# Two of four weight-splitting subtractions at the end of a decoder step move from VectorE to GpSimd

## The chip, the core and the metric

The kernel runs on one core of a Trainium2 chip. The core has TensorE (matmuls), VectorE, ScalarE and GpSimd (elementwise work), and SyncE, which issues most of the transfers; each works through a queue of its own, and they meet at semaphores. The metric is the device time of one execution in microseconds; the median of several is compared.

## What is computed

One layer of a hybrid decoder for 544 tokens (512 of a prompt and 32 of running sequences), model width 1024, all in float32. It ends with a mixture of experts and a gated embedding:

```python
x = x + mix
x = x + moe(rmsnorm(x, norm_ffn), w_router, b_router, w_up, b_up, w_down, b_down)
x = x + jax.nn.sigmoid(x @ w_ple_gate) * (p.astype(x.dtype) @ w_ple_proj)
...
y_prompt = rmsnorm(xp, norm_final)
```

The change lies around the line with `w_ple_gate`, a matrix of 1024x1024. In `moe` every token is sent to 4 of 32 experts, and the four results are weighted and added.

## The kernel before

**Split products.** A float32 product is made of faster fp32r products. A weight chunk `raw` is split: ScalarE copies it into a high part of type fp32r (`w_hi`, `gate_hi`), and VectorE subtracts that from `raw` for the low part (`w_lo`, `gate_lo`). TensorE then multiplies high by high, high by low and low by high, into the same PSUM banks.

**The experts.** The tokens (five tiles: four of 128 rows, one of 32) are gathered in blocks of 128 rows by expert. For each block 12 chunks of weights (1 MB each, 128 partitions x 2048) stream from HBM into a ring of six slots `raw`, eight for the first matrix and four for the second. A block's result goes through ScalarE into `y_rows` (line 887), and GpSimd scatters it into the table `expert_rows` in HBM by an indirect transfer (line 714). The index column `scatter_col` for it is written by VectorE (line 1635), once the scatter before has landed.

**The tail.** After the last block's steps the order is written out by hand in each engine's program:
- SyncE loads the four chunks of the gate matrix into ring slots 0 to 3 (line 579). When the last scatter has landed, it loads four rows of results per token from the table, in two halves for each tile (line 586): `yk0`, which lies in the ring slots 4 and 5 and is named `raw` in the profile, and `yk1`.
- ScalarE makes the last `w_hi` (line 849), then `gate_hi0` to `gate_hi3` (line 919) with `y_rows` and the copies `ple` between them.
- VectorE makes the last four `w_lo` (line 1541), waits for TensorE's last expert matmul, and makes the four `gate_lo` (line 1744). Between them stand `b_down_add(1)` and `b_down_add(2)` (line 1728), which add a bias sum that TensorE made in PSUM (line 1306) to `resid`. Then comes `combine(0)` (line 1763): four operations that add the weighted results of one token tile to `resid`. `gate_lo` lies in the memory of the ring slots 0 to 3, so each part overwrites its chunk.
- TensorE makes the last expert matmuls (lines 1207 and 1216), embedding products (line 1157) and bias sums (line 1306), and then, for each token tile, transposes of `resid` (line 1341, waiting for `combine`) and the gate products (lines 456, 458 and 465). Before the first of them it waits for all of `gate_hi` (semaphore `s_ghi`) and `gate_lo` (`s_glo`).
- GpSimd issues the last two scatters and then makes five tiny `rstd` operations (line 739), one for each tile, for the last norm.

Of the kernel before, what the change touches and what calls it, by code (L numbers as in the profile page):

```python
# [22 lines left out]
F32 = mybir.dt.float32  # L23
# [3 lines left out]
ALU = mybir.AluOpType  # L27
# [7 lines left out]
DN_CHUNKS = 4  # L35
# [5 lines left out]
def build(nc, x_prompt, x_sample, state_pool, p_prompt, p_sample, norm_mix, w_in, w_pool, pool_scale,  # L41
# [36 lines left out]
    with ctx:  # L78
        def sb(name, shape, dt=F32, scope=ctx):
            return scope.enter_context(nc.sbuf_tensor(name, shape, dt))  # L80

        def sem(name):
            return ctx.enter_context(nc.semaphore(name))
# [60 lines left out]
        with ExitStack() as s:  # L144
            raw = sb("raw", [P, RING, 2 * FF], scope=s)
        with ExitStack() as s:
            gate_lo = sb("gate_lo", [P, KD, D], F32R, scope=s)
# [100 lines left out]
        with ExitStack() as s:  # L248
# [7 lines left out]
            gate_hi = [sb(f"gate_hi{i}", [P, 2, D], F32R, scope=s) for i in range(2)]  # L256
# [33 lines left out]
        JOBS += [(("rank", 0), "V"), (("count", 0), "V"), (("slots", 0), "V"), (("ple", 0), "A"), (("gatesT", 0), "V")]  # L290
        assert TT == 5 and all(n % 4 != 3 for n in range(len(JOBS) - 2, len(JOBS)))
        JOB = {name: n for n, (name, _) in enumerate(JOBS)}
        EMPTIED = {}
        for n, (name, who) in enumerate(JOBS):
            EMPTIED[name] = sum(w == who for _, w in JOBS[:n + 1])
        TOTAL = {who: sum(w == who for _, w in JOBS) for who in "AV"}

        s_job = sem("job_filled")
# [92 lines left out]
        s_ghi = sem("gate_weights_hi")  # L391
        s_glo = sem("gate_weights_lo")
# [23 lines left out]
        def tail_banks(what, t):  # L416
            n = TAIL_BANK[what, t]
            return ps[:, n:n + 2, :]
# [180 lines left out]
        def _(pool):  # L599
# [109 lines left out]
            def scatter(u):  # L709
                ready = u + 1 if isinstance(u, int) else pool.to_reg(u + 1)  # L710
                pool.wait_ge(s_route, 1)
                pool.wait_ge(s_stage, ready)
                pool.wait_ge(s_y, ready)
                pool.indirect_dma_start(y4_dram[:, :], bass.IndirectOffsetOnAxis(ap=scatter_col[:, 0:1], axis=0),  # L714
                                        y_rows[:], None,
                                        bounds_check=last_row, oob_is_err=False).then_inc(s_scat, 16)

            def step(J):
                pool.wait_ge(s_stage, J if isinstance(J, int) else pool.to_reg(J))
                gather(J + 2, gather_col[:, 0:1])  # L720
                scatter(J - 1)
# [9 lines left out]
            with pool.If(n_over > 0):  # L731
                with pool.Fori(0, OVER) as b:
                    with pool.If(b < n_over):
                        step(b + (E - 1))
            scatter(n_over + (E - 2))
            scatter(n_over + (E - 1))
            for t in range(TT):
                pool.wait_ge(s_var3, t + 1)
                pool.tensor_tensor(rstd3[:, t:t + 1], var3[:, t:t + 1], half_neg[:, 0:1], ALU.pow).then_inc(s_rstd3, 1)
# [614 lines left out]
        def _(dve):  # L1354
# [93 lines left out]
            n = DB * PB  # L1448
# [276 lines left out]
            def b_down_add(t):  # L1725
                dve.wait_ge(s_bdp, t + 1)
                n = NT[t]
                dve.tensor_tensor(resid[0:n, t, :], resid[0:n, t, :], tail_banks("bd", t)[0:n].rearrange("p a n -> p (a n)"),
                                  ALU.add).then_inc(s_bd, 1)
# [9 lines left out]


            dve.wait_ge(s_lused, n_over * STEP_CHUNKS + E * STEP_CHUNKS)
            for c in range(DN_CHUNKS):
                dve.wait_ge(s_ghi, c + 1)
                dve.tensor_tensor(gate_lo[:, 2 * c:2 * c + 2, :].rearrange("p j n -> p (j n)"), raw[:, c, :],
                                  gate_hi[c][:].rearrange("p j n -> p (j n)").bitcast(F32), ALU.subtract).then_inc(s_glo, 1)
                if c % 2 == 1:
                    b_down_add((c + 1) // 2)
            tail = [0]

            def tlink(ins):  # L1750
# [78 lines left out]
```

## Time and profile before

| | us |
|---|---|
| median of three timed runs | 1469.86 (1469.83 to 1472.62) |
| the profiled execution | 1467.52 |
| its span, first to last instruction | 1465.7 |
| TensorE busy | 1419.8 |
| VectorE busy | 1225.4 |
| ScalarE busy | 927.9 |
| GpSimd busy | 210.2 |

The busy times come from one profiled execution; times inside it are counted from the start of its span. They are averages over unlike stages. The change touches only the last 100 us, so the timelines of the engines there are what has to be read. A timeline row gives start, duration, engine, line, operation, and in brackets how long the engine had stood still before and what released it. Rows of several like instructions are merged, with their count behind the x.

### The profile page before, as it was taken

The numbers are of one execution on the slowest core, as the hardware profiler recorded it, in microseconds if no ns is written. First come the engines' busy times: TensorE is split into PE (matmuls) and PEld (weight loads), VectorE is DVE, ScalarE is ACT, GpSimd is POOL, SyncE is SP. The second block draws the span as 40 slices with busy tenths as digits, with TensorE's granted clock in tenths as the row PEclk, the third lists the DMA queues.
The fourth block names the chain that finished last, engine by engine and source line by source line (L and its number), as shares of the span: only waits on it lengthen the run. The fifth ranks groups of instructions, "written<-read, shape, count | busy, mean of one in ns | idle before, by whom it ended". The sixth has DMA issues, their size and how long they took to land.

```text
span 1465.7 us, 19344 instructions
## 1 busy us (share of the span) xinstructions
PE 1419.8 (97%) x6527; PEld 1137.0 (78%) x6527; DVE 1225.4 (84%) x981; ACT 927.9 (63%) x630; POOL 210.2 (14%) x131
## 2 busy tenths in 40 slices
PE   6999978999999999999999999999999999999896
PEld 3795546888888888888888888888888888888485
DVE  2741448999999999999999999999999999999784
ACT  4310234777777777777777777777777777777422
POOL 3041000011111111111111111111111111111100
PEclk9999979999999999999999999999999999999999
DMA  9014245899999999999999999999999999999540
GB/s 313 1 61 156 73 161 222 326 362 365 383 367 374 373 371 366 369 372 369 369 369 369 370 369 371 372 376 377 373 372 376 375 374 366 367 367 362 211 173 36
DMA packets 94024, 457.31 MB, mean 312 GB/s; under 512 B 13298, under 2 KB 14878, under 8 KB 60069
## 3 DMA queue, kind: packets, MB, share of 16 engines
q1 hardware_dynamic: 84111, 437.50, 78.4%
q0 software_dynamic: 9360, 17.85, 3.2%
q10 hardware_dynamic: 526, 1.60, 0.4%
q8 instruction: 17, 0.28, 0.1%
q14 instruction: 10, 0.08, 0.0%
HBM read 451.76 MB, written 21.58 MB: 323 GB/s over the span
## 4 chain that ended last, share of the span: by engine, by line
PE 93%; DVE 2%; DMA 2%; issue 1%; ACT 1%; SPq 0%; DVEq 0%; POOLq 0%; POOL 0%; ACTq 0%
PE ps L1207 47%; PE ps L1216 23%; PE ps L1088 5%; PE ps L975 3%; PE ps L1228 2%; PE ps L1197 2%; PE ps L1190 2%; PE ps L1022 1%; PE ps L1024 1%; PE ps L1031 1%; PE ps L456 1%; PE ps L458 1%; PE ps L465 1%; DMA w_v_sb<-in_w_in_dram 1%; PE ps L1103 1%
## 5 line engine op out<-in xcount | busy, mean ns | idle before, releaser
L1541 DVE TENSOR_TENSOR w_lo<-raw,w_hi 128x2048 fp32r<-128x2048 f32 x384 | 867.5, 2286 | 66.4 <-PE ps L1216 60.9
L849 ACT ACTIVATE w_hi<-raw 128x2048 fp32r<-128x2048 f32 x384 | 732.1, 1916 | 216.5 <-PE ps L1207 179.7
L1207 PE MATMUL ps<-w_hi,xT_hi 128*128 128x512 f32 x1024 | 278.8, 394 | 0.0
L1207 PE MATMUL ps<-w_hi,xT_lo 128*128 128x512 f32 x1024 | 275.2, 391 | 0.0
L1216 PE MATMUL ps<-w_lo,xT_hi 128*128 128x512 f32 x1024 | 273.8, 389 | 0.0
L1207 PEld LDWEIGHTS ps<-w_hi,xT_lo 128*128 128x128 f32 x1024 | 192.9, 188 | 41.4
L1216 PEld LDWEIGHTS ps<-w_lo,xT_hi 128*128 128x128 f32 x1024 | 192.3, 188 | 40.0
L1207 PEld LDWEIGHTS ps<-w_hi,xT_hi 128*128 128x128 f32 x1024 | 191.0, 189 | 38.5
L714 POOL DMA_INDIRECT expert_rows<-y_rows,scatter_col x32 | 137.4, 4294 | 406.3 <-ACT y_rows L887 406.3
L1207 PE MATMUL ps<-w_hi,aT_hi 128*128 128x512 f32 x512 | 139.9, 395 | 0.0
L1216 PE MATMUL ps<-w_lo,aT_hi 128*128 128x512 f32 x512 | 137.0, 389 | 0.4 <-DVE w_lo L1541 0.4
L1207 PE MATMUL ps<-w_hi,aT_lo 128*128 128x512 f32 x512 | 136.8, 389 | 0.0
L1216 PEld LDWEIGHTS ps<-w_lo,aT_hi 128*128 128x128 f32 x512 | 96.0, 188 | 20.6 <-DVE w_lo L1541 0.8
L1207 PEld LDWEIGHTS ps<-w_hi,aT_lo 128*128 128x128 f32 x512 | 96.1, 188 | 20.1
L706 POOL DMA_INDIRECT x_rows<-xn_rows,gather_col x30 | 30.5, 1016 | 553.5 <-PE ps L1190 518.6
L1207 PEld LDWEIGHTS ps<-w_hi,aT_hi 128*128 128x128 f32 x512 | 93.9, 188 | 17.8
L887 ACT ACTIVATE y_rows<-ps 128x1024 f32<-128x1024 f32 x32 | 32.9, 1028 | 79.1 <-PE ps L1216 79.1
L1660 DVE TENSOR_SCALAR glu<-ps 128x1024 f32<-128x1024 f32 x32 | 39.2, 1224 | 13.8 <-PE ps L1216 13.8
L1518 DVE TENSOR_TENSOR resid<-resid,ps 128x512 f32<-128x512 f32 (+1 forms) x10 | 6.4, 680 | 51.4 <-PE ps L1088 51.4
L1655 DVE TENSOR_TENSOR aT_lo<-ps,aT_hi 128x1024 fp32r<-128x1024 f32 x32 | 39.0, 1217 | 3.3 <-ACT aT_hi L877 3.3
L1228 PE MATMUL ps<-bias_hl,oh_up 128*128 128x512 f32 x128 | 36.1, 404 | 4.4 <-DVE xT_lo L1599 2.6
L975 PE MATMUL ps<-w_v_sb,xT 128*128 128x512 f32 x80 | 38.3, 634 | 1.9 <-DMA w_v_sb<-in_w_in_dram 1.6
(250 smaller groups left out, 1216.5 us busy)
## 6 DMA issues: line engine op xcount, KB each, us to landing
raw<-in_w_up_dram SPq DMA_DIRECT2D x256, 1024.0 KB, 5.8
raw<-in_w_down_dram SPq DMA_DIRECT2D x128, 1024.0 KB, 7.7
raw<-in_w_ple_gate_dram SPq DMA_DIRECT2D x4, 1024.0 KB, 5.4
raw<-expert_rows SPq DMA_DIRECT2D x4, 1024.0 KB, 7.2
yk<-expert_rows SPq DMA_DIRECT2D x4, 1024.0 KB, 10.3
resid<-in_x_prompt_dram SPq DMA_DIRECT2D x4, 512.0 KB, 10.1
w_v_sb<-in_w_in_dram SPq DMA_DIRECT2D x2, 1024.0 KB, 9.4
w_z_sb<-in_w_in_dram SPq DMA_DIRECT2D x2, 1024.0 KB, 12.7
```

Source lines behind the costliest of these rows:

```text
L706: pool.indirect_dma_start(x_rows[:], None, xn_dram[:, :], bass.IndirectOffsetOnAxis(ap=col, axis=0), bounds_check=last_token, oob_is_err=F ...
L714: pool.indirect_dma_start(y4_dram[:, :], bass.IndirectOffsetOnAxis(ap=scatter_col[:, 0:1], axis=0), y_rows[:], None, bounds_check=last_row ...
L849: act.activation(w_hi[:, s % SPLIT, :], raw[:, s % RING, :], ACT.Copy).then_inc(s_hi, 1)
L887: act.activation(y_rows[:], dn, ACT.Copy).then_inc(s_y, 1)
L975: mm = pe.matmul(bank(name), xT[:, k, t * P:(t + 1) * P], w_v_sb[:, k, :], start=(k == 0), stop=(k == KD - 1))
L1088: mm = pe.matmul(bank(name, b)[0:n, :], rows_k, w, start=(k == 0), stop=(k == KD - 1), skip_group_check=True)
L1207: mm = pe.matmul(out[:, c:c + 512], (xh, xl)[xs], w_hi[:, s % SPLIT, base + c:base + c + 512], start=(fresh and xs == 0 and base == 0), st ...
L1216: mm = pe.matmul(out[:, c:c + 512], xh, w_lo[:, s % SPLIT, base + c:base + c + 512], start=False, stop=last and k == len(parts) - 1, skip_ ...
L1228: pe.matmul(gu[:, c:c + 512], oh_up[:], bias_hl[:, c:c + 512], start=True, stop=False, skip_group_check=True)
L1541: dve.tensor_tensor(w_lo[:, s % SPLIT, :], raw[:, s % RING, :], w_hi[:, s % SPLIT, :].bitcast(F32), ALU.subtract).then_inc(s_lo, 1)
L1655: dve.tensor_tensor(aT_lo[:].rearrange("p k n -> p (k n)"), tp, aT_hi[:].rearrange("p k n -> p (k n)").bitcast(F32), ALU.subtract).then_in ...
L1660: dve.tensor_scalar(glu[:], gu[:, 0:FF], LIMIT, None, ALU.min).then_inc(s_glu, 1)
```

## The change

GpSimd gets a function `gate_low(c)`, the same subtraction that VectorE makes, on the same memory. It is called for chunk 1 between GpSimd's last two scatters, and for chunk 3 behind the last scatter. VectorE makes only chunks 0 and 2, each followed by its `b_down_add`.

```diff
             scatter(n_over + (E - 2))
+
+            def gate_low(c):
+                pool.wait_ge(s_ghi, c + 1)
+                pool.tensor_tensor(gate_lo[:, 2 * c:2 * c + 2, :].rearrange("p j n -> p (j n)"), raw[:, c, :],
+                                   gate_hi[c][:].rearrange("p j n -> p (j n)").bitcast(F32), ALU.subtract).then_inc(s_glo, 1)
+
+            gate_low(1)
             scatter(n_over + (E - 1))
+            gate_low(3)
             for t in range(TT):
...
             dve.wait_ge(s_lused, n_over * STEP_CHUNKS + E * STEP_CHUNKS)
-            for c in range(DN_CHUNKS):
+            for c in range(0, DN_CHUNKS, 2):
                 dve.wait_ge(s_ghi, c + 1)
                 dve.tensor_tensor(gate_lo[:, 2 * c:2 * c + 2, :].rearrange("p j n -> p (j n)"), raw[:, c, :],
                                   gate_hi[c][:].rearrange("p j n -> p (j n)").bitcast(F32), ALU.subtract).then_inc(s_glo, 1)
-                if c % 2 == 1:
-                    b_down_add((c + 1) // 2)
+                b_down_add(c // 2 + 1)
```

The end of GpSimd's queue, before and after in one piece; the DMA rows are the last two scatters:

```order
 L710 REGISTER_ALU
 L714 DMA expert_rows<-y_rows,scatter_col 2176x1024
+L739 TENSOR_TENSOR gate_lo<-raw,gate_hi 128x2048
 L710 REGISTER_ALU
 L714 DMA expert_rows<-y_rows,scatter_col 2176x1024
-L739 TENSOR_TENSOR rstd<-var,half_neg 128x1 x5
+L739 TENSOR_TENSOR gate_lo<-raw,gate_hi 128x2048
+L747 TENSOR_TENSOR rstd<-var,half_neg 128x1 x5
```

The first new operation stands ahead of the last scatter, and needs only ScalarE's `gate_hi1`; the second stands behind the scatter. Neither waits for VectorE or TensorE.

VectorE's queue from the last `w_lo` to `combine(0)`, in the kernel before:

```order
L1635 COPY scatter_col<-code_of 128x1
L421 REGISTER_ALU [waits chunk_lo_used]
L1541 TENSOR_TENSOR w_lo<-raw,w_hi 128x2048 [waits chunk_hi]
L1741 ISA
L1744 TENSOR_TENSOR gate_lo<-raw,gate_hi 128x2048 [waits gate_weights_hi,chunk_lo_used]
L1744 TENSOR_TENSOR gate_lo<-raw,gate_hi 128x2048 [waits gate_weights_hi]
L1728 TENSOR_TENSOR resid<-resid,ps 128x1024 [waits b_down_summed]
L1744 TENSOR_TENSOR gate_lo<-raw,gate_hi 128x2048 [waits gate_weights_hi] x2
L1728 TENSOR_TENSOR resid<-resid,ps 128x1024 [waits b_down_summed]
L1763 SCALAR_TENSOR_TENSOR resid<-raw_5,topw,resid 128x1024 [waits expert_rows_landed_0_0]
```

and the same stretch in the changed kernel, eight lines further down in the file:

```order
L1643 COPY scatter_col<-code_of 128x1
L421 REGISTER_ALU [waits chunk_lo_used]
L1549 TENSOR_TENSOR w_lo<-raw,w_hi 128x2048 [waits chunk_hi]
L1749 ISA
L1752 TENSOR_TENSOR gate_lo<-raw,gate_hi 128x2048 [waits gate_weights_hi,chunk_lo_used]
L1736 TENSOR_TENSOR resid<-resid,ps 128x1024 [waits b_down_summed]
L1752 TENSOR_TENSOR gate_lo<-raw,gate_hi 128x2048 [waits gate_weights_hi]
L1736 TENSOR_TENSOR resid<-resid,ps 128x1024 [waits b_down_summed]
L1770 SCALAR_TENSOR_TENSOR resid<-raw_5,topw,resid 128x1024 [waits expert_rows_landed_0_0]
```

Two of the four `gate_lo` are gone; the rest keeps its order, and the first still waits for TensorE's last use of a low part (`chunk_lo_used`), which GpSimd's new first operation does not.

## Rows read from the trace of the kernel before

**Rows 1.** The page, part 1: busy us, share, instructions by engine.

```profile
PE 1419.8 (97%) x6527; PEld 1137.0 (78%) x6527; DVE 1225.4 (84%) x981; ACT 927.9 (63%) x630; POOL 210.2 (14%) x131
```

**Rows 2.** Chain that ended last, 1350 to 1466 us: start, us, what.

```profile
1362.57 8.83 DMA expert_rows<-y_rows,scatter_col
1371.66 2.30 DVE w_lo L1541
1374.00 1.21 PE ps L1216 x4
```

**Rows 3.** Window of the gate stage: length, TensorE busy, granted clock, DMA share, GB/s.

```profile
1410.00:1455.00 45.00, 44.54 (x209) 1.00 0.12 48
```

**Rows 4.** Timeline of VectorE, 1371 to 1392 us.

```profile
1371.66 2.29 DVE L1541 TENSOR_TENSOR w_lo<-raw,w_hi 128x2048 fp32r<-128x2048 f32 x1
1375.24 4.50 DVE L1744 TENSOR_TENSOR gate_lo<-raw,gate_hi 128x2048 fp32r<-128x2048 f32 x2 [1.29 <-PE ps L1216]
1379.65 1.22 DVE L1728 TENSOR_TENSOR resid<-resid,ps 128x1024 f32<-128x1024 f32 x1
1380.78 4.49 DVE L1744 TENSOR_TENSOR gate_lo<-raw,gate_hi 128x2048 fp32r<-128x2048 f32 x2
...
1386.32 5.24 DVE L1763 SCALAR_TENSOR_TENSOR resid<-raw,topw,resid 128x1024 f32<-128x1024 f32 x4
```

**Rows 5.** Timeline of TensorE, 1357 to 1394 us.

```profile
1357.68 1.09 PE L1197 MATMUL ps<-ident,lin 128*128 128x128 f32 x8 [2.73 <-issue]
...
1372.52 1.07 PE L1216 MATMUL ps<-w_lo,aT_hi 128*128 128x512 f32 x4
1374.00 1.20 PE L1216 MATMUL ps<-w_lo,aT_hi 128*128 128x512 f32 x4 [0.42 <-DVE w_lo L1541]
...
1378.07 1.02 PE L1306 MATMUL ps<-bias_hl,gatesT 128*128 128x512 f32 x2
...
1391.70 1.94 PE L1341 MATMUL ps<-ident,resid 128*128 128x128 f32 x8 [4.04 <-DVE resid L1763]
```

**Rows 6.** Timelines of GpSimd and SyncE: the last scatter's issue, the first loads behind.

```profile
1377.13 1.25 POOL L714 DMA_INDIRECT expert_rows<-y_rows,scatter_col  x1 [11.96 <-ACT y_rows L887]
...
1380.61 0.81 SPq L586 DMA_DIRECT2D raw<-expert_rows  x2
```

**Rows 7.** DMA issues of 1380.0 to 1380.9 us: count, KB, us to landing.

```profile
raw<-expert_rows SPq DMA_DIRECT2D x1, 1024.0 KB, 5.2
```

**Rows 8.** Timeline of ScalarE, 1367 to 1382 us.

```profile
1367.29 3.70 ACT L919 ACTIVATE gate_hi<-raw 128x2048 fp32r<-128x2048 f32 x2
...
1375.32 1.02 ACT L887 ACTIVATE y_rows<-ps 128x1024 f32<-128x1024 f32 x1 [3.43 <-PE ps L1216]
...
1379.59 1.90 ACT L919 ACTIVATE gate_hi<-raw 128x2048 fp32r<-128x2048 f32 x1
```

**Rows 9.** GpSimd's instructions grouped by line and shape: busy us, mean ns.

```profile
L676 POOL TENSOR_TENSOR sumA<-ext 128x687 f32<-128x687 f32 x2 | 2.7, 1334 | 8.2 <-DVE diff L1398 8.2
...
L676 POOL TENSOR_TENSOR sumA<-sumB 128x673 f32<-128x673 f32 x1 | 1.6, 1627 | 0.1
```

**Rows 10.** Timelines of GpSimd and VectorE, 91 to 110 us.

```profile
91.62 1.33 POOL L676 TENSOR_TENSOR sumA<-ext 128x687 f32<-128x687 f32 x1 [8.16 <-DVE diff L1398]
93.03 1.69 POOL L676 TENSOR_TENSOR sumB<-sumA 128x685 f32<-128x685 f32 x1
...
92.18 1.35 DVE L1434 TENSOR_TENSOR uT<-gated,uT 128x544 f32<-128x544 f32 x1
...
109.25 0.72 DVE L1434 TENSOR_TENSOR uT<-gated,uT 128x544 f32<-128x544 f32 x1
```

**Rows 11.** Windows, columns as in rows 3, around TensorE's idle time before 1391.70.

```profile
1390.50:1391.00 0.50, 0.00 (x0) 0.96 0.97 410
1391.00:1391.70 0.70, 0.00 (x0) 0.50 1.07 445
...
1397.50:1398.00 0.50, 0.50 (x3) 0.71 0.93 393
```

## The prediction

> **What bounds the kernel now.** I read the page's busy shares first, then the chain of waits over the last 115 us, then the engines' timelines there. TensorE is busy for 97% of the span [rows 1], so nothing outside its queue matters except where that queue stands still, and the change touches only the last 100 us. There the chain of waits runs through the landing of the scatter before the last one, VectorE's last `w_lo`, TensorE's matmuls on it, and then VectorE's gate parts [rows 2, 4]. From 1410 to 1455 us TensorE is busy for 44.54 of 45 us, at the full clock [rows 3]: a shift at the head of the gate stage reaches the end of the kernel unchanged, and nothing in that stage gives it back.
>
> The head of the gate stage is `combine(0)`, four VectorE operations from 1386.32 us [rows 4], behind which TensorE stands idle for 4.04 us before it transposes `resid` at 1391.70 [rows 5]. Three things must be there for `combine(0)`: VectorE's own queue, free at 1386.3; the bank sums of TensorE (line 1306) for `b_down_add`; and the first half of `yk0`. That half is issued at 1380.61 and lands 5.2 us later, so at **1385.8 us** [rows 6, 7]. So the queue of VectorE is late by only 0.5 us against the transfer behind it. This is the first number to see: however much work leaves VectorE, `combine(0)` can't start before 1385.8 us unless the last scatter goes earlier, and that one waits for `y_rows` at 1375.32 + 1.02 us on ScalarE [rows 8], thus for TensorE's last matmuls at 1374.00 [rows 5].
>
> **The change, part by part.** It takes two `gate_lo` operations out of VectorE's run: the four take 4.50 + 4.49 us [rows 4], two of them some 4.5 us. By the above at most 0.5 us of this can come back. It adds two operations of 128x2048 to GpSimd. No row shows this size there; the nearest are the window sums with 128x687 in 1.334 us and 128x673 in 1.627 us [rows 9]. Scaled by elements they give 1.334 x 2048/687 = **3.98 us** and 1.627 x 2048/673 = 4.95 us; with a fixed part left out of the scaling (0.25 us, an estimate: what falls off if a quarter of a microsecond of the 1.334 doesn't grow) 3.5 us. I take 3.98, since of the ten sums seven take 1.32 to 1.34 us, two wait for VectorE (below), and only the one of 1.63 has no such reason, and keep 3.5 and 4.95 as ends.
>
> The GPSIMD Engine Reference of the Trainium skill (section 3.1) gives 4497 ns for a 2048-element fp32 `tensor_tensor` on GpSimd. By that the sum below would be about 4.4 us instead of 3.3; no row here has that size.
>
> **What the two engines do to each other.** This decides the sign. VectorE's `uT` product of 128x544, with both inputs in SBUF, takes 0.72 us at 109.25, when GpSimd does nothing, but 1.35 us at 92.18, where GpSimd's sum of 91.62 to 92.95 is under way [rows 10]. It ends at 93.53, so 0.58 us behind GpSimd's end: its own 0.72 less 0.14 of start-up. GpSimd's next sum, started at 93.03, takes 1.69 and not 1.33, and ends 1.19 us after VectorE's end (1.33 less 0.14). The pattern stands twice, 8.5 us apart, with the same lengths. So in these rows the two engines never work on such operands together: the second waits for the first, whole.
>
> Now the first GpSimd part. It waits for `gate_hi1`, which ScalarE ends at 1367.29 + 3.70 = 1370.99 [rows 8]. GpSimd is idle then (its previous scatter issue was long over). It starts at about **1371.1**. VectorE's last `w_lo` starts at 1371.66, once the scatter that had been under way has landed [rows 2, 4]. It too has two SBUF inputs. So GpSimd has 0.55 us of lead, on the one operation that the chain runs through: GpSimd ends at 1371.1 + 3.98 = 1375.1, and `w_lo` at 1375.1 + (2.29 - 0.14) = **1377.25**, where it was 1373.95. That is 3.3 us on the chain.
>
> Behind it everything keeps its distance and moves by 3.3: TensorE's last four matmuls from 1374.00 to 1377.3; `y_rows` ends 1379.6; the scatter issue (queued on GpSimd behind the new operation, but long free of it) from 1377.13 [rows 6] to 1380.4; the first half of `yk0` lands at 1385.8 + 3.3 = 1389.1.
>
> The second way to `combine(0)` is VectorE's. `gate_lo0` from 1378.5 to 1380.8. `b_down_add(1)` needs the bank sum that ended at 1378.07 + 1.02 = 1379.1 [rows 5], now 1382.4: it ends at 1383.6. `gate_lo2` 1383.5 to 1385.8. GpSimd's second part waits for `gate_hi3`, ended at 1379.59 + 1.90 = 1381.5 [rows 8], now 1384.8, so in the middle of `gate_lo2`: it gets its turn at 1385.8 and ends at 1389.65. `b_down_add(2)` reads PSUM and runs beside it. The first `combine` (two SBUF inputs) ends 1389.65 + 1.15 = 1390.8; before it ended at 1386.32 + 1.28 = 1387.6. That is **3.2 us**, as much as the landing gives (1389.1 against 1385.8). The sum is 3.3 us.
>
> For 3.5 us an operation the same steps give 2.3 to 2.8; for 4.95 the first wait gives 4.3 and the second part ends at 1391.6, so 5.2. The five short `pow` operations of GpSimd and the rest of its queue stand far behind; nothing else waits there. The profiled execution was 1467.52 us, with a span of 1465.7, and would become 1470.8; the median of the timed runs was 1469.86, which becomes **1473.2 us**.
>
> **The rivals.**
> (a) *The two engines work side by side*: the change does what its words say. `w_lo` stays at 1371.66 and GpSimd's parts are over by 1375.1 and 1385.5, before anyone asks for them (TensorE asks at 1394.75). `combine(0)` then waits only for `yk0`: 1385.8 instead of 1386.32, or 0.5 us less, 1469.3 us. This is the case on the other side, not slower; it decides whether GpSimd's read excludes VectorE's. Against it stand both pairs of lengths [rows 10]. The page SBUF — State Buffer of the Trainium skill (section "SBUF: two separate sides") says of the shared pair that "whichever ... starts first gets the pair for the whole instruction", with which the 1.35 and the 1.69 us agree; by it this rival is out.
> (b) *VectorE comes first.* If the earlier scatter lands 0.6 us sooner, or GpSimd takes up its wait 0.6 us later, `w_lo` keeps its place and GpSimd waits until 1373.95, and ends at 1377.8. The last scatter then goes 0.7 to 1.1 us later than at 1377.13, `gate_lo0` waits to 1377.8 and ends 1379.95, `gate_lo2` ends 1383.3, GpSimd's second part 1387.15, the first `combine` 1388.3: 0.7 to 1.1 us more, 1470.8 us. The landing of the earlier scatter, 8.83 us [rows 2], is a long one, and it is the margin.
> (c) *The clock falls too.* TensorE now stands from 1373.5 to 1377.3, 3.7 us, where it stood for 0.42 [rows 5]. In its idle time after 1387.67 the granted clock was 0.96 in 1390.5 to 1391.0 and 0.50 right after, so it fell 3.3 us into the idle time, to 1.2 GHz, and it was back at 2.4 GHz in 1397.5 to 1398.0 (0.71 over that half) [rows 11]. If that repeats, some 6 us of TensorE's queue run at half speed, 3.05 us more for the bank sums: `gate_lo2` ends at 1388.9, GpSimd's second part at 1392.75, the first `combine` at 1393.9. That is 6.3 us, 1476.2 us. Against it: TensorE was idle for 2.73 us before 1357.68 [rows 5] and its next eight transposes took 1.09 us, where at the low clock eight take 1.94, and one case is thin ground for 3.7.
> (d) *The operation on GpSimd is far slower than scaled* (the output is of type fp32r, which no GpSimd row has): each further microsecond in it counts once in the first wait and about once more in the second; at 6 us it is some 7.5 us, 1477.4 us.
>
> **How the numbers follow.** Forecast (GpSimd first, clock kept, 3.5 to 4.95 us an operation: 1472.2 to 1475.1 us) 0.57; (c) 0.18; (b) 0.13; (a) 0.08; (d) 0.04. The time is the forecast's, 1473.2. The range takes in (b) and most of (c): 1470.5 to 1477.0; (a), (d) and the upper part of (c) stay out. A change of 0.2%, 2.9 us, is about what a measurement can tell from none; the bound is 1472.8, close under the forecast. Slower than that: most of the forecast, 0.42, with (c) and (d), together 0.63. Within 0.2%: the short end of the forecast, (b) and (a), 0.35. Faster by 0.2% would need 2.9 us where 0.5 can be had: 0.02.
>
> **What would show it.** In the profile of the changed kernel: VectorE's `w_lo` before TensorE's last line-1216 matmuls with a duration of some 5.5 us instead of 2.29 (or a start that late), ending 2.15 us after GpSimd's; GpSimd's `gate_lo` near 4.0 us; the last scatter issued near 1380.4; the first `combine` stretched to the end of GpSimd's second part; an unchanged distance from the transposes to the end. A `w_lo` of 2.29 us beside a running GpSimd operation would overthrow the forecast; a `w_lo` that starts before GpSimd's would make it (b).

## The result

The changed kernel took 1473.20 us (median of 20 runs, 1469.90 to 1477.08), the kernel before 1471.01 us (20 runs, 1467.93 to 1472.62). The ratio is **1.0017, 95% interval 1.0009 to 1.0024**: 1.3 to 3.5 us slower, about 2.5; the two medians lie 2.2 us apart. A second set of runs of the same kernel (below, `again`) gave 1.0024, interval 1.0012 to 1.0037. The predicted time was 1473.2 us, so the time came out on the spot. That is partly luck: the forecast was 3.3 us added to a median of three runs, 1469.86, which lay 1.15 us below the median of twenty, and two of its steps were not those of the execution profiled. The experiments take them apart.

The ends of the queues of GpSimd and VectorE in the changed kernel (timeline: start, duration, engine, line, operation, idle time before and what ended it), which answer to [rows 4] and [rows 6]:

```profile
1373.51 5.75 POOL L739 TENSOR_TENSOR gate_lo<-raw,gate_hi 128x2048 fp32r<-128x2048 f32 x1 [7.14 <-ACT gate_hi L927]
1379.41 2.85 POOL L714 DMA_INDIRECT expert_rows<-y_rows,scatter_col  x1 [0.16 <-issue]
1383.30 5.83 POOL L739 TENSOR_TENSOR gate_lo<-raw,gate_hi 128x2048 fp32r<-128x2048 f32 x1 [1.04 <-ACT gate_hi L927]
```

```profile
1372.55 2.29 DVE L1549 TENSOR_TENSOR w_lo<-raw,w_hi 128x2048 fp32r<-128x2048 f32 x1
1376.96 4.44 DVE L1752 TENSOR_TENSOR gate_lo<-raw,gate_hi 128x2048 fp32r<-128x2048 f32 x1 [2.13 <-PE ps L1224]
1381.33 1.21 DVE L1736 TENSOR_TENSOR resid<-resid,ps 128x1024 f32<-128x1024 f32 x1
1382.46 2.28 DVE L1752 TENSOR_TENSOR gate_lo<-raw,gate_hi 128x2048 fp32r<-128x2048 f32 x1
1384.76 1.22 DVE L1736 TENSOR_TENSOR resid<-resid,ps 128x1024 f32<-128x1024 f32 x1
1389.73 5.25 DVE L1770 SCALAR_TENSOR_TENSOR resid<-raw,topw,resid 128x1024 f32<-128x1024 f32 x4 [3.75 <-DMA raw<-expert_rows]
```

Every overlap of two operations with two inputs in SBUF is a wait here. GpSimd starts at 1373.51 while `w_lo` runs to 1374.84, and takes 5.75 us: 1.33 beside `w_lo` and 4.42 behind it. It ends at 1379.26. VectorE's `gate_lo0`, which is 2.29 us of work, shows 4.44 us and ends at 1381.40, 2.14 us behind GpSimd's end, as the 0.58 us in [rows 10] foretold (the operation less 0.14). GpSimd's second part again carries 1.44 us beside `gate_lo2`. The adds of `b_down_add`, which read one input from PSUM, are not held up: 1.22 us at 1384.76, in the middle of GpSimd's second part.

In this execution VectorE's `w_lo` came first by 0.96 us, so TensorE's matmuls and `y_rows` lost nothing. What was lost is in the scatter. ScalarE ended `y_rows` at 1378.07:

```profile
1377.05 1.02 ACT L895 ACTIVATE y_rows<-ps 128x1024 f32<-128x1024 f32 x1 [2.72 <-PE ps L1224]
```

GpSimd was then still at its new operation, the scatter started at 1379.41, and its issue took 2.85 us where it was 1.25 [rows 6]. `combine(0)` stood 3.75 us for the data. The freed VectorE time is there (it is done at 1386.0, 3.75 us ahead of the data that land at 1389.7) and is worth nothing.

### The profile page after: what moved, and what is told of

It reads as the page before. It is cut to its first block, busy times and chain, and to the rows that moved or that the text cites. A ratio compares the mean times of both kernels' runs of the same rounds, so it can differ in the third digit from the quotient of the medians.

```text
span 1470.5 us, 19344 instructions
## 1 busy us (share of the span) xinstructions
PE 1424.0 (97%) x6527; PEld 1140.0 (78%) x6527; DVE 1223.5 (83%) x979; ACT 928.2 (63%) x630; POOL 223.5 (15%) x133
## 4 chain that ended last, share of the span: by engine, by line
PE 93%; issue 2%; DMA 2%; DVE 2%; ACT 1%; POOL 1%; SPq 0%; DVEq 0%; POOLq 0%; ACTq 0%
PE ps L1215 47%; PE ps L1224 23%; PE ps L1096 5%; PE ps L983 3%; PE ps L1236 2%; PE ps L1205 2%; PE ps L1198 2%; PE ps L1030 1%; PE ps L456 1%; PE ps L1032 1%; PE ps L1039 1%; PE ps L458 1%; PE ps L465 1%; DMA w_v_sb<-in_w_in_dram 1%; PE ps L1111 1%
```

## The executions come in two kinds

Before the experiments can be read, one thing about the executions: ahead of this stretch TensorE pauses for 2.7 to 3.0 us. In the profiled execution of the kernel before, the clock was kept over that pause ([rows 5], eight transposes in 1.09 us). In the changed kernel's it was not. The same line in the changed kernel, and in a second profile of the kernel before (`before_2`):

```profile
1357.22 1.96 PE L1205 MATMUL ps<-ident,lin 128*128 128x128 f32 x8 [2.87 <-issue]
```

```profile
1357.42 1.97 PE L1197 MATMUL ps<-ident,lin 128*128 128x128 f32 x8 [2.72 <-issue]
```

The windows of `before_2` (length, TensorE busy, granted clock, DMA share, GB/s) show the two levels, 2.4 and 1.2 GHz:

```profile
1357.00:1358.00 1.00, 0.58 (x3) 0.50 0.97 401
1362.00:1363.00 1.00, 1.00 (x2) 0.50 0.01 4
1364.00:1365.00 1.00, 1.00 (x4) 1.00 0.00 0
```

Of 13 profiles of all kernels, 10 show the fall here and 3 don't, so it does not belong to the change; the profile that the prediction had was of the rarer kind. The length of the pause doesn't tell the kinds apart: it was 2.72 us in `before_2`, where the clock fell, and 2.89 in `extra_write`, where it was kept. The kind matters, since, counted from the transposes, it makes `y_rows` 2.2 us later, `gate_hi1` 2.9, and the `w_lo` behind the scatter index only 1.4. In the rare kind `gate_hi1` is there at 1370.99 and `w_lo` starts at 1371.66: GpSimd first. In the common kind `gate_hi1` is there at 1373.43 and `w_lo` starts at 1372.55: VectorE first.

```diff
(before_2, before_3: the kernel before; after_3: the changed kernel; no edit)
```

> The kernel before, for another profile. In the profiles so far the clock fell at TensorE's pause of 2.7 to 3.0 us before its transposes of lin in some executions of the changed kernels and not in the one of the kernel before. If that fall belongs to the execution and not to the change, it shows here too in some profile, and then the transposes of resid start 35 to 36.5 us behind those of lin instead of 34.0; the changed kernel's 37.9 is to be held against that. Without a fall: 34.0 again.

> The same kernel for a third profile: 34.0 us from the transposes of lin to those of resid where the clock is kept, 35 to 36.5 where it fell ahead of them.

> The changed kernel for a third profile. If the clock fell ahead of the transposes of lin, gate_hi1 is late and VectorE's w_lo comes first, then w_lo keeps 2.29 us, the last scatter and gate_lo0 are late, 37.9 us from transposes to transposes. If it was kept, GpSimd comes first, w_lo shows 5.5 to 6.1 us, TensorE's second pause follows, and the distance is 38 to 41.3.

All three fell as the first branch says. The distances below are the measure for all experiments: from the start of the transposes of `lin` to the start of `y_rows`, on to the first transposes of `resid`, and from those to the end of the span. Each kernel is to be held against the kernel before of its own kind; the last column is the difference from `lin` to the end.

| profile | clock at `lin` | `lin` to `y_rows` | `lin` to `resid` | `resid` to end | against before |
|---|---|---|---|---|---|
| before | kept | 17.6 | 34.0 | 74.0 | |
| extra_write | kept | 17.7 | 34.1 | 73.9 | 0.0 |
| again (the change) | kept | 22.4 | 41.3 | 75.3 | +8.6 |
| before_2 | fell | 19.9 | 36.2 | 74.3 | |
| before_3 | fell | 19.8 | 36.2 | 74.4 | |
| after (the change) | fell | 19.8 | 37.9 | 75.4 | +2.7 |
| after_3 (the change) | fell | 19.8 | 37.6 | 75.5 | +2.5 |
| only_chunk1 | fell | 19.8 | 38.4 | 75.0 | +2.9 |
| only_chunk3 | fell | 19.8 | 37.1 | 74.2 | +0.7 |
| both_behind | fell | 19.8 | 40.5 | 74.2 | +4.1 |
| chunk0_and_3 | fell | 22.6 | 39.4 | 74.7 | +3.5 |
| extra_read | fell | 20.2 | 37.3 | 74.0 | +0.7 |
| early_gate | fell | 19.8 | 35.2 | 74.6 | -0.8 |

So in the common kind the change costs 1.4 to 1.7 us up to `resid`, and some 1.0 behind it, where the stretch at the low clock is longer: about 10 us instead of the 7 that end in [rows 11]. The windows of the changed kernel:

```profile
1394.00:1395.00 1.00, 0.00 (x0) 0.50 1.00 418
...
1403.00:1404.00 1.00, 1.00 (x4) 0.50 1.11 279
1404.00:1405.00 1.00, 1.00 (x6) 0.91 0.91 360
```

The sum, 2.5 to 2.7 us, agrees with the measured 2.5, which is taken over executions of both kinds.

The idle time of TensorE ahead of the transposes of `resid` is longer in the changed kernel (5.72 us in `after`, 4.03 in `before_2`), but its length alone does not give the longer stretch: behind 4.97 us of it in only_chunk3 the stretch is about 7 us, behind 4.46 us in `again` and 4.48 in chunk0_and_3 it is about 10. What decides it, these runs don't show.

## The experiments

The theory: an operation with two inputs in SBUF on either engine holds back one of the other until it is over, and which one the change hurts depends on who comes first. The rivals: the scatter is late only by its place behind a new operation in GpSimd's queue; or only the clock makes the difference.

**again.** The changed kernel, unedited, timed and profiled again.

> The changed kernel once more, for a second profile of it. Turn-taking theory (an operation of one engine with two inputs in SBUF holds back one of the other engine until it is over): GpSimd's two gate parts each show 4.4 us plus the time that VectorE was ahead of them, and VectorE's overlapped operations show their 2.15 us behind GpSimd's end; 1.3 to 3.3 us slower than the kernel before, by which engine comes first at the last w_lo. Rival (the queue alone: the last scatter is late because it stands behind a new operation, and the engines don't hold each other): all of VectorE's operations show 2.29 us. Rival (clock alone: the loss is TensorE's lower clock in idle time that some executions have): the time to combine(0) is that of the kernel before where the clock kept up.

Measured: 1474.33 us against 1470.17, ratio 1.0024 (1.0012 to 1.0037). Its profile is of the rare kind. It begins with the first step of the forecast and goes on as rival (c). GpSimd, then VectorE, then TensorE:

```profile
1371.31 4.55 POOL L739 TENSOR_TENSOR gate_lo<-raw,gate_hi 128x2048 fp32r<-128x2048 f32 x1 [5.92 <-ACT gate_hi L927]
1382.07 1.25 POOL L714 DMA_INDIRECT expert_rows<-y_rows,scatter_col  x1 [6.21 <-ACT y_rows L895]
1388.63 5.37 POOL L739 TENSOR_TENSOR gate_lo<-raw,gate_hi 128x2048 fp32r<-128x2048 f32 x1 [5.30 <-ACT gate_hi L927]
```

```profile
1371.94 6.07 DVE L1549 TENSOR_TENSOR w_lo<-raw,w_hi 128x2048 fp32r<-128x2048 f32 x1
1380.17 2.29 DVE L1752 TENSOR_TENSOR gate_lo<-raw,gate_hi 128x2048 fp32r<-128x2048 f32 x1 [2.17 <-PE ps L1224]
...
1391.22 7.82 DVE L1770 SCALAR_TENSOR_TENSOR resid<-raw,topw,resid 128x1024 f32<-128x1024 f32 x4
```

```profile
1378.06 2.07 PE L1224 MATMUL ps<-w_lo,aT_hi 128*128 128x512 f32 x4 [4.24 <-DVE w_lo L1549]
1379.93 5.75 PE L1165 MATMUL ps<-w_proj_sb,pT 128*128 128x512 f32 x8
```

GpSimd leads by 0.63 us, `w_lo` shows 6.07 us and ends at 1378.01, 2.15 behind GpSimd's 1375.86. The four adds of `combine(0)` show 7.82 us instead of 5.24 [rows 4], since GpSimd's second part runs to 1394.00. Then rival (c) came: TensorE stood for 4.24 us, four matmuls then took 2.07 us (1.20 before, [rows 5]) and the granted clock was 0.72 in 1377 to 1378 and 0.50 behind it. This execution's span, 1474.5 us, is among the longest. That both kinds have the two-input operations in turn, and that the time to `combine(0)` is not that of before in either, goes against both rivals.

**only_chunk1, only_chunk3, both_behind.** One operation alone, and both behind the last scatter.

```diff
 only_chunk1
             gate_low(1)
             scatter(n_over + (E - 1))
-            gate_low(3)
 only_chunk3
-            gate_low(1)
             scatter(n_over + (E - 1))
             gate_low(3)
 both_behind
-            gate_low(1)
             scatter(n_over + (E - 1))
+            gate_low(1)
             gate_low(3)
```

(VectorE makes the chunks that are left, `b_down_add(1)` after the first or second and `b_down_add(2)` after the last of them.)

> Only chunk 1 on GpSimd, ahead of the last scatter; VectorE makes 0, 2 and 3. Turn-taking: nearly the whole loss, 1.5 to 3.0 us slower than before, because this is the operation that holds back either w_lo or the last scatter's issue and gate_lo0. Queue alone: the same sign, but 0.6 us at most (GpSimd's 4.4 us from 1371.1 end before the scatter is due at 1377.13; only when gate_hi1 comes late does it reach past). Clock alone: no difference from before.

> Only chunk 3 on GpSimd, behind the last scatter; VectorE makes 0, 1 and 2. Turn-taking: GpSimd is ready at 1381.5, waits for gate_lo2 to end at 1383.1, runs to 1387.4, and combine(0) waits for it although its data landed at 1385.8: the first combine ends 1388.6 instead of 1387.6, 0.9 us slower. Queue alone: nothing stands behind it but the small pow operations, and VectorE has one operation less: combine(0) at its landing, 0.5 us faster. Clock alone: no difference.

> Both operations on GpSimd, both behind the last scatter. Turn-taking: the scatter is issued as before, but GpSimd's operations run from 1378.4 and hold back gate_lo2 and then combine(0), to 1389.4 if they alternate: 1.5 to 3.0 us slower. Queue alone: the scatter is free again, VectorE has two operations less: 0.5 us faster than before. Clock alone: no difference.

Measured: only_chunk1 1.0025 (1.0016 to 1.0034), 2.4 to 5.0 us slower: as much as the whole change, within the noise. In its profile the scatter before the last landed some 0.8 us later than in `after`, which is part of the 2.9 us in the table. only_chunk3 1.0007 (0.9998 to 1.0016); its profile shows the 0.9 us expected. GpSimd's part and `combine(0)` in it:

```profile
1384.37 5.88 POOL L739 TENSOR_TENSOR gate_lo<-raw,gate_hi 128x2048 fp32r<-128x2048 f32 x1 [3.20 <-ACT gate_hi L926]
```

```profile
1388.67 6.62 DVE L1770 SCALAR_TENSOR_TENSOR resid<-raw,topw,resid 128x1024 f32<-128x1024 f32 x4 [1.62 <-DMA raw<-expert_rows]
```

The data landed at 1388.7, but the first add ran only after GpSimd's end at 1390.25: 6.62 us for four adds of 1.3. The queue rival had this kernel 0.5 us faster; it isn't.

both_behind, with the scatter free in front of both operations (again 1.25 us, at 1379.01), is no better for it: 1.0029 (1.0016 to 1.0041). Under the queue rival it had to be the best. More than the 1.5 to 3.0 us I had expected, too, and the reason is new:

```profile
1380.27 9.03 POOL L739 TENSOR_TENSOR gate_lo<-raw,gate_hi 128x2048 fp32r<-128x2048 f32 x2
```

```profile
1382.15 9.31 DVE L1752 TENSOR_TENSOR gate_lo<-raw,gate_hi 128x2048 fp32r<-128x2048 f32 x1
```

VectorE's `gate_lo2` came during the first GpSimd operation (4.52 us, to 1384.8), and GpSimd's second one (4.58 us), which followed at once, since the semaphore that it waits for had long been set, went ahead of it: 9.31 us for 2.29 of work, ending 2.16 us behind GpSimd's 1389.30. I had let the engines alternate. In the extra_read kernel below the second GpSimd operation waits for a semaphore that the first one sets at its end, and there VectorE came in between.

**chunk0_and_3.** GpSimd takes chunk 0 and not chunk 1, so that it comes first at `w_lo` whatever the clock did.

```diff
-            gate_low(1)
+            gate_low(0)
             scatter(n_over + (E - 1))
             gate_low(3)
```

> As the change, but GpSimd takes chunk 0 instead of chunk 1, ahead of the last scatter, so that it can start 1.85 us sooner, at about 1369.3, and surely ahead of VectorE's last w_lo at 1371.66. Turn-taking: GpSimd holds until 1373.7, w_lo ends at 1375.9 instead of 1373.95, so 1.9 us more for TensorE's last matmuls and for y_rows; the second part as in the change: 2 to 3.5 us slower than before. w_lo shows more than 4 us or starts at GpSimd's end. Queue alone: the operation is over 3 us before the scatter is due, so no loss, up to 0.5 us faster.

Measured: 1.0036 (1.0022 to 1.0049), 3.2 to 7.2 us slower, the highest ratio of all, though its interval overlaps those of the others that lose. GpSimd from 1372.70 for 4.60 us; `w_lo`:

```profile
1373.45 6.00 DVE L1549 TENSOR_TENSOR w_lo<-raw,w_hi 128x2048 fp32r<-128x2048 f32 x1
```

`y_rows` starts 22.6 us behind the transposes of `lin` instead of 19.8: 2.8 us through `w_lo`, though GpSimd's operation was over at 1377.30, well before the scatter (issue 1.25 us, at 1382.63). This is the forecast's first step isolated, in the common kind of execution and with the clock kept: TensorE stood for 2.49 us and its next four matmuls took 1.19.

**extra_read, extra_write.** The disputed cost by itself: the kernel before, all four parts on VectorE, with unneeded work on GpSimd, once with two reads per element and once with writes only.

```diff
             scatter(n_over + (E - 2))
+            pool.wait_ge(s_ghi, 1)
+            room = p_sb[:].rearrange("p t n -> p (t n)")
+            high = gate_hi[0][:].rearrange("p j n -> p (j n)").bitcast(F32)[:, 0:TT * PD]
+            for _ in range(2):
+                link(pool.tensor_tensor(room, high, high, ALU.subtract))
             scatter(n_over + (E - 1))
 (extra_write)
+            for _ in range(5):
+                link(pool.memset(room, 0.0))
```

> The kernel before with all four gate parts on VectorE, and two more operations on GpSimd ahead of the last scatter, each a subtraction of 128x1280 with both inputs from gate_hi0 (its result is not used), 2.8 us each, from about 1369.3. Turn-taking: the second one meets w_lo; w_lo or the GpSimd operation is stretched by the overlap, w_lo ends up to 3 us later: 1.5 to 3 us slower than before. No holding back: w_lo keeps 2.29 us, and the time is that of the kernel before, since GpSimd is free again by 1375.1, ahead of the scatter at 1377.13.

> The same with five memsets of 128x1280 on GpSimd, 1.1 us each, which only write, in place of the two subtractions: GpSimd is busy about as long, from 1369.3 to 1375.5. If it is GpSimd's reading that excludes VectorE's second input, w_lo keeps 2.29 us and the time is that of the kernel before. If any GpSimd operation on SBUF excludes it, w_lo is stretched by up to 1.1 us.

Measured: extra_read 1.0014 (1.0002 to 1.0025), 0.3 to 3.7 us slower with no work moved. GpSimd's two operations in it, and its `w_lo` and first two `gate_lo`, each held behind one of them:

```profile
1371.58 6.64 POOL L740 TENSOR_TENSOR p_sb<-gate_hi 128x1280 f32<-128x1280 f32 x2 [5.21 <-ACT gate_hi L924]
```

```profile
1373.22 2.82 DVE L1546 TENSOR_TENSOR w_lo<-raw,w_hi 128x2048 fp32r<-128x2048 f32 x1
1377.35 5.22 DVE L1749 TENSOR_TENSOR gate_lo<-raw,gate_hi 128x2048 fp32r<-128x2048 f32 x2 [1.30 <-PE ps L1221]
```

The effect in the profile, 0.7 us, is less than the 1.5 to 3 us expected: the first GpSimd operation took 2.32 us, not 2.8, and VectorE was held up by only 0.53 us at `w_lo` and 0.73 at `gate_lo0`.

extra_write 1.0007 (0.9998 to 1.0016), no difference that the runs can tell, and in its profile five memsets run over the whole of `w_lo` without touching it:

```profile
1368.03 6.08 POOL L739 MEMSET p_sb<- 128x1280 f32 x5 [4.09 <-ACT gate_hi L923]
```

```profile
1370.51 2.29 DVE L1545 TENSOR_TENSOR w_lo<-raw,w_hi 128x2048 fp32r<-128x2048 f32 x1
```

So GpSimd's writing does not exclude VectorE's second input, and an operation that reads does; one with a single input on GpSimd was not tried. The page SBUF — State Buffer of the Trainium skill (section "Who interferes with whom") says the same, that a two-input VectorE instruction contends with a GpSimd instruction that reads SBUF, "not with one that only writes it"; the 2.29 us beside the memsets and the 6.07 beside the subtraction agree.

**early_gate.** A try at a faster kernel, all on VectorE: its idle time ahead of the scatter index is used, and the wait for TensorE's last low product goes. `gate_low(c)` is here a function of VectorE, with the subtraction of chunk `c`; the loop over the chunks is gone.

```diff
-                if x == 2:
-                    stage_scatter(J).then_inc(s_stage, 1)
...
-            dve.wait_ge(s_lused, n_over * STEP_CHUNKS + E * STEP_CHUNKS)
...
+            gate_low(0)
+            stage_scatter(J).then_inc(s_stage, 1)
+            gate_low(1)
+            gate_low(2)
+            b_down_add(1)
+            gate_low(3)
+            b_down_add(2)
```

> All four gate parts on VectorE. Its last w_lo no longer stands behind the scatter index, gate_lo0 is made before the index and gate_lo1 right behind it, without the wait for TensorE's last low product, in time in which VectorE stood idle; gate_lo2 goes ahead of b_down_add(1). If the chain to combine(0) runs through w_lo, y_rows, the scatter's issue and the landing, TensorE's wait of 0.42 us goes, and the last scatter is issued beside an idle VectorE in 0.9 us instead of 1.25: landing 0.8 us earlier, and combine(0) starts at the landing, 1.3 us sooner in all: 0.5 to 1.5 us faster than before. If VectorE's queue were what counts, the same order would give 4 us and more.

Measured: 1.0004 (0.9995 to 1.0013), no difference. The scatter was issued beside an idle VectorE in 0.97 us, as expected, and the profile has `resid` 1.0 us earlier than the kernel before of its kind; of the 1.3 us the 0.42 was not to be had, because `y_rows` stands at 19.8 us with or without the edit where the clock fell. A gain of 1.3 us lies outside the interval, whose end is at 0.7 us; one of 0.8 us, as the single profile has it from `lin` to the end, is at its edge and stays open. No version here beats the kernel before.

## Why the prediction was right, point by point

- **Nothing to gain** (0.5 us at most, since `combine(0)` waits for its data): held. VectorE was free 3.75 us before the data in the changed kernel, and only_chunk3, which takes work off VectorE behind the scatter alone, was not faster.
- **The engines take turns**: held, in every overlap of the eight profiles with a reading operation on GpSimd. A held VectorE operation ended 2.14 to 2.16 us behind GpSimd's, so the 0.14 us read from [rows 10] is exact to 0.02 there; a held GpSimd part ended 4.39 to 4.44 us behind VectorE's. What was not foreseen is that the one that waits can be passed over a second time (both_behind).
- **Who is first at `w_lo`**: the step that failed for most executions. The 0.55 us of lead came from one profile, and that was of the rarer kind. The chances were 0.57 + 0.18 for GpSimd first and 0.13 for VectorE first; of three profiles of the changed kernel two were VectorE first. It came first for neither of the reasons that rival (b) names: the landing, called a long one there, took much the same in all profiles (the index column follows the issue by 8.6 to 9.4 us, 8.96 in the kernel before). What moved was `gate_hi1`, 2.9 us later behind the fallen clock. Where GpSimd was first, `w_lo` ended at 1378.0 instead of 1377.25, mostly by the longer GpSimd operation.
- **The forecast's own branch**, GpSimd first and the clock kept through TensorE's pause, stands in none of the three profiles of the changed kernel: two are (b), one is (c). Only its steps are shown, in `again` and chunk0_and_3.
- **The size of a GpSimd part**: 3.98 us was taken, 4.4 to 4.6 measured (4.55 where nothing was in its way, 4.52 and 4.58 in both_behind). It is inside 3.5 to 4.95, and the 4497 ns that the GPSIMD Engine Reference of the Trainium skill (section 3.1) gives was the better figure. Scaling by elements from 687 was 13% short; scaled from the 2.32 us of 128x1280 in extra_read it would be 3.7 us, so a GpSimd operation's time doesn't follow from its size alone. Both shorter ones read twice from one tile, the gate part from two; whether that is the reason was not tried.
- **Rival (b) had 0.7 to 1.1 us**; the common kind costs 2.5 to 2.7. Two terms were missing. The issue of the scatter itself waits for VectorE: 2.85 us in place of 1.25, 1.6 us. And the distance from the transposes to the end was taken as unchanged, but the stretch at the low clock before the gate stage got longer, 1.0 us. The first could have been read from the kernel before, whose last two issues are 2.60 and 1.25 us long.
- **Rival (c), the clock in the pause**: real, in `again` (4.24 us of idle, then 1.2 GHz), but only where GpSimd is first. 6.3 us were estimated for it, 8.6 measured, with the longer operation (twice 0.5 us) and the longer low stretch at the end (1.3).
- **The total**: the forecast of +3.3 stood for the rare kind and was too low for it (8.6); the common kind, priced too low as (b), costs 2.5 to 2.7. Added to the first, low, median of before (1469.86; 1471.01 over 20 runs) the 3.3 gave the measured 1473.2. The sign, the turn-taking and the missing gain were understood; that the number hit to the tenth is luck. And 0.63 on slower by over 0.2% was high: the ratio came out at 1.0017, then at 1.0024.

## What to carry to other kernels

Moving an elementwise operation with two inputs in SBUF from VectorE to GpSimd gives no parallelism with other such operations of VectorE: the work becomes a queue over both engines, at twice the length (4.5 against 2.29 us), and whoever needs the other engine's next result pays for it. Find what the freed engine waits for next before counting its relief as a gain; here it was a transfer, which waits for a scatter that GpSimd itself issues. A lead of half a microsecond read from one profile is not an order: take a second profile before building on it.

## What the runs showed of the hardware

- **The issue of an indirect scatter on GpSimd waits for VectorE's two-input operation too.** That it waits is inferred from the ends: for the last two scatters of every profile, wherever such an operation was under way, the issue ended 0.85 to 0.89 us behind its end. In `before_2` 1379.09 + 1.25 = 1380.34 with the first of these two `gate_lo` over at 1379.49 (each 2.29 us), in the changed kernel 1382.26 with `gate_lo0` over at 1381.40. Beside an idle VectorE it takes 0.97 us (early_gate).

```profile
1379.09 1.25 POOL L714 DMA_INDIRECT expert_rows<-y_rows,scatter_col  x1 [12.52 <-ACT y_rows L887]
```

```profile
1377.20 4.49 DVE L1744 TENSOR_TENSOR gate_lo<-raw,gate_hi 128x2048 fp32r<-128x2048 f32 x2 [2.11 <-PE ps L1216]
```

```profile
1381.32 0.97 POOL L714 DMA_INDIRECT expert_rows<-y_rows,scatter_col  x1 [12.49 <-ACT y_rows L887]
```

It can wait for more than one. In the kernel before, 30 of the 32 issues take 4.45 us or more; the one at 404.79 starts beside a `w_lo` that ends at 406.16 and is over at 409.24, 0.88 us behind the end of the next `w_lo`. Why the last ones got through at the first end is not shown.

```profile
L714 POOL DMA_INDIRECT expert_rows<-y_rows,scatter_col x32: 1250/4451/4516, 298.5 to 1377.1; - x32
```

- **Two GpSimd operations that follow each other at once were not parted** (both_behind, one case): VectorE's waiting operation showed 9.31 us instead of 2.29. Where the second waited for the end of the first through a semaphore (extra_read), VectorE came in after the first.
- **Memsets on GpSimd cost VectorE nothing**: `w_lo` took 2.29 us within a run of five of them (extra_write).
- **The same kernel has two timelines in its last 110 us**, by whether TensorE's clock fell from 2.4 to 1.2 GHz in a pause of 2.7 to 3.0 us. It shifted the order of two engines by 1.5 us, and so which operation of the change paid.
